# A hybrid decoder step on one core: 24 more weight units of the input projection taken in high and low halves, the low half made by an accumulating DMA

## The chip, the core and the metric

The kernel runs on one core of one Trainium2 chip. Its time is the device time of one execution in microseconds (us); smaller is better. A result is the median of several executions.

## What is computed

Two layers of a decoder trunk, for 256 prompt positions and 8 sample positions together (264 columns). The part that the change touches is the input projection of each layer, `proj = xn @ w_in`, and beside it the state-space scan and the search for the cut of the top 256 keys:

```
xn = rmsnorm(x, norm_mix)
proj = xn @ w_in                     # 2048 -> 8448 padded columns
u, q, k, v, qi, ki, wi, gl = jnp.split(proj, ...)
y_att = attend(q, k, v, qi, ki, wi, pos)          # top-256 keys by indexer score
y_ssm, h_re, h_im = s5_scan(u, h0_re, h0_im, a_re, a_im, log_dt, b_re, b_im, c_re, c_im, d)
gates = jax.nn.sigmoid(gl).reshape(nb, s, N_BRANCH, D_MODEL)
x = x + (gates[:, :, 0] * (y_ssm' @ w_branch[0]) + gates[:, :, 1] * (y_att @ w_branch[1])) @ w_out
x = x + (jax.nn.silu(gate) * up) @ w_ffn_down     # gate, up = split(rmsnorm(x) @ w_ffn_up)
```

All inputs and outputs are fp32.

## The kernel before

**Units.** The weights are streamed from DRAM in units of 128 x 1024 fp32 (512 KB): eight 128 x 128 blocks, eight matmuls' worth, against 264 columns. Units 0 to 131 are `w_in` (two units to a block of 128 output columns, so block f is units 2f and 2f+1), 132 to 203 the GLU, branch and output weights. SyncE loads unit u into slot u % 6 of `ring` once unit u-6 is done (`units` reaches u-5); `u_in[u % 6]` tells that it has landed.

**Two ways to multiply.** A plain unit is one fp32 matmul for each block (L608; the trace has two records for each). A split unit (those in `SPLIT`: 8 to 55, fourteen from 92 to 105, all from 132) is three fp32r matmuls for each block (L604, L605, L606): high weights by high activations, high by low, low by high. ScalarE copies the raw unit to fp32r, which makes the high part (`highs_to`, L1021), and VectorE subtracts it from the raw unit, which makes the low part (`lows_to`, L1311). `w_low` lies at the same addresses as `ring`: the low part is written over the raw one. Units 56 to 91 are plain, since VectorE has other work there.

**The stretch around units 56 to 87.** TensorE takes one unit and then one small matmul (L757), the count of the bisection for the top-256 cut: it waits for `count_ready`, which VectorE gives (L1467), and releases `total_ready`, for which VectorE waits (L1484). VectorE works through the scan of the first half of the states (`scan(0, bisect)`, tensor_tensor instructions L1541, L1549, L1550, L1551, later L1584, L1592, L1593) and puts one step of the bisection between two steps of the scan. Loop n of the count follows unit 56+n. ScalarE only evacuates a block's PSUM bank when its two units are done (L1031, from block 34 on L1045 as a tanh); there are four banks. GpSimd issues nothing from the last fetch of indexer keys (eight, behind units of the first part) until the gathers of keys after the scan of the second half (L1867).

Of the kernel before, what the change touches and what calls it, by code (L numbers as in the profile page):

```python
# [10 lines left out]
ALU = mybir.AluOpType  # L11
# [3 lines left out]
P = 128  # L15
# [98 lines left out]
def build(nc, d, o):  # L114
    with ExitStack() as ctx:
# [214 lines left out]
        def unit_w(u):  # L330

            if u in LATE:
                raw, low = (a[:, u % 6, :].rearrange("p (c n) -> p c n", c=2) for a in (ring, wlow))
                return raw, late_high[LATE[u]], low
            at = HIGH_AT[u % 4]
            return ring[:, u % 6, :], (wih if u < G_GLU else wmh)[:, at:at + KT8], wlow[:, u % 6, :]

        def weight(a, u, k):
            return a[:, k // 4, k % 4 * P:k % 4 * P + P] if u in LATE else a[:, k * P:(k + 1) * P]

        def high_free(u):

            if u in LATE:
                return max((n + 1 for n in LATE if n < u and LATE[n] == LATE[u]), default=0)
# [22 lines left out]
        kg_in = [ctx.enter_context(nc.semaphore(f"kg_in{i}")) for i in range(NS)]  # L367
        vg_in = [ctx.enter_context(nc.semaphore(f"vg_in{i}")) for i in range(NS)]
        cleared = []

        def sem(name):
# [39 lines left out]
        count_ready, total_ready = sem("count_ready"), sem("total_ready")  # L411
        ties_counted, ties_placed, picked, picks_placed = sem("ties_counted"), sem("ties_placed"), sem("picked"), sem("picks_placed")
        per_seq_ready, spread_ready, spread_used, gix_ready = (
            sem("per_seq_ready"), sem("spread_ready"), sem("spread_used"), sem("gather_rows_ready"))
        q_spread, v_out = sem("q_spread"), sem("v_out")
# [84 lines left out]
        for layer in range(DEPTH):  # L500
            with nc.Block() as block:
                def landed(u):
                    return 16 * (G_END // 6 * layer + u // 6 + 1)

                def attend_units(u):
                    return (22 * u + 9) // 18
# [77 lines left out]
                def _(pe):  # L584
                    mm = nc.tensor.matmul

                    def unit_part(u, seq, c, full, high, low, k0, n, opens, closes, made=None):

                        if k0 == 0:
                            if opens:  # L590
                                pe.wait_ge(bank_free[seq % 4], seq // 4 + 1)
                            if u in SPLIT:
                                pe.wait_ge(unit_low, lows_by(u))
                            else:
                                pe.wait_ge(u_in[u % 6], landed(u))
                        out = main[seq % 4][:, 0:T]
                        raw, wh, wl = unit_w(u)
                        for k in range(k0, k0 + n):
                            if made:
                                made(8 * c + k)  # L600
                            kk = 8 * c + k
                            starts, stops = opens and k == 0, closes and k == 7
                            if u in SPLIT:
# [163 lines left out]
                    fill(3)  # L767
                    pe.wait_ge(ties_counted, 1)
                    mm(side[0][:, 1:2], same_seq, n_above, start=True, stop=True)
                    mm(side[0][:, 2:3], before_seq, n_equal, start=True, stop=True).then_inc(ties_placed, 1)  # L770
                    fill(1)
                    pe.wait_ge(picked, 1)
                    mm(side[0][:, 3:4], before_seq, prefix[:, P:NK], start=True, stop=True)
                    mm(side[0][0:NS, 4:5], is_seq, above[:, P:NK], start=True, stop=True).then_inc(picks_placed, 1)
                    fill(1)
                    pe.wait_ge(per_seq_ready, 1)
                    for h in range(2):
# [224 lines left out]
                def _(act):  # L1002
# [6 lines left out]
                    def highs_to(last):  # L1009

                        nonlocal next_high
                        while next_high <= last:
                            u = next_high
                            next_high += 1
                            if u not in SPLIT:
                                continue
                            raw, high, _ = unit_w(u)
# [276 lines left out]
                def _(dve):  # L1294
# [194 lines left out]
                    def pick():  # L1489
# [3 lines left out]
                        st.link(tsc(equal, score, tau, 0.0, ALU.is_equal, ALU.add, accum_out=n_equal))  # L1493
                        dve.sem_inc(ties_counted, 1)
                        st.link(v.tensor_tensor_scan(prefix, ones[:, 0:1].to_broadcast([P, NK]), equal, 0.0, ALU.mult, ALU.add))
                        dve.wait_ge(ties_placed, 1)
# [4 lines left out]
                        v.tensor_tensor_scan(prefix, ones[:, 0:1].to_broadcast([P, NK]), above, 0.0, ALU.mult, ALU.add).then_inc(picked, 1)  # L1501
                        dve.wait_ge(picked, 1)
                        lows_to(92)
                        dve.wait_ge(picks_placed, 1)
                        st.mark(v.tensor_copy(by_rank[:, NK:NK + 1], page_row[:]))
# [6 lines left out]
                        st.link(stt(rank_of, ranks, seg_first, rank_of, ALU.is_ge, ALU.mult))  # L1512
                        dve.sem_inc(per_seq_ready, 1)
                        lows_to(93)
# [315 lines left out]
                def _(pool):  # L1830
# [187 lines left out]
```

## Time and profile before

| | us |
|---|---|
| runs of the kernel before | 3126.95, 3127.31, 3134.06 |
| their median | 3127.31 |
| the profiled execution | 3135.18 |
| its span, first to last instruction | 3133.4 |
| TensorE busy (share of the span) | 3058.2 (98%) |
| VectorE, ScalarE, GpSimd busy | 1949.7, 1193.2, 236.4 |
| units 60 to 83 of layer 0, start of 60 to start of 84 | 88.1 |

The profiled execution is 0.25% above the median, and 1.8 us of it lie around the span. Matmuls are pipelined: their recorded durations overlap, so what a unit takes is read from the starts of two matmuls that stand a unit apart, and not from durations. Busy time of a line says what the engine did there; whether it costs time is told by who waits for whom.

### The profile page before, as it was taken

Reading aid. Unit: us, or ns where it says so; the run is one execution under the profiler, and the core shown is the slowest. Engines: PE = TensorE matmul, PEld = TensorE weight load, DVE = VectorE, ACT = ScalarE, POOL = GpSimd, SP = SyncE. Lnnn points to the kernel's source line nnn. Section 1 sums busy time; section 2 is a strip of 40 time slices with the busy share of each in tenths; the row PEclk is TensorE's granted clock in tenths of the full one; section 3 lists DMA queues with packets and bytes.
Section 4 is the critical chain, followed back from the end, with each engine's and each line's share of the span. In section 5 each row is a group of like instructions: output and inputs, shape, how many; then the busy total and the mean of one; then the engine's idle time right before and its main releaser. Section 6 shows DMA issues by size and latency. Waiting matters only on the chain. (4 is left out here: it accounts for less than half of the span.)

```text
span 3133.4 us, 58534 instructions
## 1 busy us (share of the span) xinstructions
PE 3058.2 (98%) x23384; PEld 2895.2 (92%) x23384; DVE 1949.7 (62%) x3387; ACT 1193.2 (38%) x1689; POOL 236.4 (8%) x219
## 2 busy tenths in 40 slices
PE   8999999999999999999999999999999999999999
PEld 7988777999999999999988887788999999999999
DVE  7558769557655545555575686785676555455553
ACT  4440233434545333334334302334445543333332
POOL 4330000300000000000033200004000000000000
PEclk9999999999999999999999999999999999999999
DMA  7444334655555655556554443347455556555564
GB/s 253 160 147 142 121 110 142 225 172 171 192 179 182 200 169 173 181 181 202 188 191 162 143 142 120 106 147 238 159 179 188 182 180 200 168 174 183 179 207 131
DMA packets 147888, 538.06 MB, mean 172 GB/s; under 512 B 19569, under 2 KB 24817, under 8 KB 147217
## 3 DMA queue, kind: packets, MB, share of 16 engines
q1 hardware_dynamic: 137872, 509.50, 48.9%
q0 software_dynamic: 9216, 25.18, 2.6%
q8 instruction: 111, 1.82, 0.2%
q10 hardware_dynamic: 640, 1.16, 0.1%
q14 instruction: 49, 0.39, 0.0%
HBM read 528.56 MB, written 7.21 MB: 171 GB/s over the span
## 5 line engine op out<-in xcount | busy, mean ns | idle before, releaser
L1750 DVE TENSOR_TENSOR w_ffn_low<-ring_ffn,w_ffn_high 128x1024 fp32r<-128x1024 f32 (+1 forms) x480 | 638.5, 1331 | 464.2 <-ACT w_ffn_high L1256 464.2
L985 PE MATMUL main<-x_ffn_high,w_ffn_high 128*128 128x264 f32 x2816 | 799.3, 284 | 0.0
L986 PE MATMUL main<-x_ffn_low,w_ffn_high 128*128 128x264 f32 x2816 | 797.7, 283 | 0.0
L987 PE MATMUL main<-x_ffn_high,w_ffn_low 128*128 128x264 f32 x2816 | 797.3, 283 | 0.0
L1256 ACT ACTIVATE w_ffn_high<-ring_ffn 128x1024 fp32r<-128x1024 f32 (+1 forms) x480 | 547.9, 1142 | 653.6 <-PE main L987 652.5
L986 PEld LDWEIGHTS main<-x_ffn_low,w_ffn_high 128*128 128x128 f32 x2816 | 530.7, 188 | 0.1
L985 PEld LDWEIGHTS main<-x_ffn_high,w_ffn_high 128*128 128x128 f32 x2816 | 530.3, 188 | 0.1
L987 PEld LDWEIGHTS main<-x_ffn_high,w_ffn_low 128*128 128x128 f32 x2816 | 527.8, 187 | 0.0
L608 PE MATMUL main<-xn,ring 128*128 128x264 f32 x2112 | 484.7, 389 | 0.0
L608 PEld LDWEIGHTS main<-xn,ring 128*128 128x128 f32 x2112 | 394.3, 190 | 65.5 <-issue 0.8
L985 PE MATMUL main<-hidden_high,w_ffn_high 128*128 128x264 f32 x1408 | 400.9, 285 | 0.0
L987 PE MATMUL main<-hidden_high,w_ffn_low 128*128 128x264 f32 x1408 | 399.9, 284 | 0.0
L986 PE MATMUL main<-hidden_low,w_ffn_high 128*128 128x264 f32 x1408 | 398.7, 283 | 0.0
L606 PE MATMUL main<-x_high,w_low 128*128 128x264 f32 x992 | 283.4, 286 | 0.0
L985 PEld LDWEIGHTS main<-hidden_high,w_ffn_high 128*128 128x128 f32 x1408 | 265.1, 188 | 0.0
L987 PEld LDWEIGHTS main<-hidden_high,w_ffn_low 128*128 128x128 f32 x1408 | 265.0, 188 | 0.0
L986 PEld LDWEIGHTS main<-hidden_low,w_ffn_high 128*128 128x128 f32 x1408 | 264.7, 188 | 0.0
L1311 DVE TENSOR_TENSOR w_low<-ring,w_mid_high 128x1024 fp32r<-128x1024 f32 x144 | 175.5, 1225 | 94.3 <-ACT w_mid_high L1021 87.8
L604 PE MATMUL main<-x_high,w_in_high 128*128 128x264 f32 x768 | 226.2, 294 | 4.6 <-DVE w_low L1311 4.3
L605 PE MATMUL main<-x_low,w_in_high 128*128 128x264 f32 x768 | 218.1, 284 | 0.0
L1021 ACT ACTIVATE w_mid_high<-ring 128x1024 fp32r<-128x1024 f32 x144 | 150.6, 1051 | 101.5 <-PE main L606 89.9
L606 PEld LDWEIGHTS main<-x_high,w_low 128*128 128x128 f32 x992 | 188.9, 190 | 0.0
(373 smaller groups left out, 4614.8 us busy)
## 6 DMA issues: line engine op xcount, KB each, us to landing
ring_ffn<-in_w_up SPq DMA_DIRECT2D x352, 512.0 KB, 3.2
ring<-in_w_in SPq DMA_DIRECT2D x264, 512.0 KB
ring_ffn<-in_w_down SPq DMA_DIRECT2D x128, 704.0 KB, 4.1
ring<-in_w_br SPq DMA_DIRECT2D x64, 512.0 KB
ring<-in_w_out SPq DMA_DIRECT2D x64, 512.0 KB
ring<-in_w_glu SPq DMA_DIRECT2D x16, 512.0 KB
out_x<-x SPq DMA_DIRECT2D x8, 528.0 KB, 5.8
x<-in_x SPq DMA_DIRECT2D x4, 528.0 KB, 5.3
```

The costliest lines, as they stand in the source:

```text
L604: mm(out, weight(wh, u, k), high[:, kk, :], start=starts, stop=False)
L605: mm(out, weight(wh, u, k), low[:, kk, :], start=False, stop=False)
L606: m = mm(out, weight(wl, u, k), high[:, kk, :], start=False, stop=stops)
L608: m = mm(out, weight(raw, u, k), full[:, kk, :], start=starts, stop=stops)
L985: mm(out, wfh[:, slot, w], high[:, kk, :], start=kk == 0, stop=False)
L986: mm(out, wfh[:, slot, w], low[:, kk, :], start=False, stop=False)
L987: m = mm(out, wfl[:, slot, w], high[:, kk, :], start=False, stop=kk == chunks * kts - 1)
L1021: af(high, raw, ACT.Copy).then_inc(unit_high, 1)
L1256: af(wfh[:, s, 0:cols], ring_ffn[:, s, 0:cols], ACT.Copy).then_inc(high_ready, 1)
L1311: tt(low, raw, high.bitcast(F32), ALU.subtract).then_inc(unit_low, 1)
L1750: tt(wfl[:, s, 0:cols], ring_ffn[:, s, 0:cols], wfh[:, s, 0:cols].bitcast(F32), ALU.subtract).then_inc(low_ready, 1)
```

## The change

Units 60 to 83 of each layer (`ADDED`) become split units. VectorE has no part in it. ScalarE writes the high part (fp32r copy) into a buffer of its own, and then the negated copy (scale -1) over the raw unit in its slot; that releases `less_high`. GpSimd issues a DMA for each unit which reads the raw unit from DRAM a second time and adds it (`accum_op=ALU.add`) onto the negated highs, so that the slot holds raw minus high, the low part. Its end releases `low_added[u % 2]`, on which TensorE starts the unit. The DMA of unit u waits for the end of that of unit u-2. There are three buffers for highs; unit u from 63 on may be taken by ScalarE when `units` reaches u-2, which is when unit u-3 is done. In `evac_gates` ScalarE now makes the highs of up to unit 2f+4 before it evacuates block f. The other lines of the diff put several semaphores into one (`pick_step`, `placed`), with the same order of waits.

```diff
+ADDED = range(60, 84)
...
+            if u in ADDED and u % 3 == 2:
+                raw, low = (a[:, u % 6, :].rearrange("p (c n) -> p c n", c=2) for a in (ring, wlow))
+                return raw, late_high[0], low
+            at = HIGH_AT[2 + u % 3 if u in ADDED else u % 4]
...
         def high_free(u):
 
+            if u in ADDED:
+                return u - 2 if u >= ADDED[3] else 56
...
+                def added_by(u):
+                    return 16 * (len(ADDED) // 2 * layer + (u - ADDED[0]) // 2 + 1)
...
+                            if u in ADDED:
+                                pe.wait_ge(low_added[u % 2], added_by(u))
+                            elif u in SPLIT:
...
-                            if u in SPLIT:
+                            if u in SPLIT or u in ADDED:
                                 mm(out, weight(wh, u, k), high[:, kk, :], start=starts, stop=False)
...
-                            af(high, raw, ACT.Copy).then_inc(unit_high, 1)
+                            if u in ADDED:
+                                af(high, raw, ACT.Copy)
+                                af(low, raw, ACT.Copy, scale=-1.0).then_inc(less_high, 1)
+                            else:
+                                af(high, raw, ACT.Copy).then_inc(unit_high, 1)
...
                     def evac_gates(first, count):
                         for f in range(first, first + count):
+                            highs_to(min(2 * f + 4, ADDED[-1]))
                             act.wait_ge(units, 2 * f + 2)
...
+                    for u in ADDED:
+                        n = u - ADDED[0]
+                        pool.wait_ge(less_high, n + 1)
+                        if n >= 2:
+                            pool.wait_ge(low_added[u % 2], added_by(u - 2))
+                        g.dma_start(unit_w(u)[2], d["w_in"][layer, u] if u % 3 < 2 else d["w_in"][layer, u].rearrange("p (c n) -> p c n", c=2),
+                                    accum_op=ALU.add).then_inc(low_added[u % 2], 16)
                     pool.wait_ge(gix_ready, 1)
```

ScalarE's instructions in layer 0, from the last split unit before the stretch into the evacuations of blocks 28 and on. Before:

```order
L1021 ACTIVATE w_in_high<-ring 128x1024 [waits units_done,unit_weights_in1,pi_done]
L1115 ACTIVATE arena<-side 128x264 [waits bu_ready] x20
L1031 ACTIVATE proj<-main 128x264 [waits units_done]
L1115 ACTIVATE arena<-side 128x264 [waits bu_ready] x12
L1031 ACTIVATE proj<-main 128x264 [waits units_done] x7
```

And in the changed kernel (its line 1049 is L1031 of before; `main` is the PSUM bank of a block):

```order
L1134 ACTIVATE arena<-side 128x264 [waits bu_ready] x12
L1049 ACTIVATE proj<-main 128x264 [waits units_done]
L1036 ACTIVATE w_in_high<-ring 128x1024 [waits units_done,unit_weights_in0]
L1037 ACTIVATE w_low<-ring 128x1024
L1049 ACTIVATE proj<-main 128x264 [waits units_done]
L1036 ACTIVATE w_in_high<-ring 128x1024 [waits units_done,unit_weights_in1]
L1037 ACTIVATE w_low<-ring 128x1024
L1036 ACTIVATE w_in_high_b<-ring 128x2x512 [waits units_done,unit_weights_in2]
L1037 ACTIVATE w_low<-ring 128x1024
L1049 ACTIVATE proj<-main 128x264 [waits units_done]
```

Between two evacuations there now stand two pairs of copies, one pair for each unit. On GpSimd, behind the last fetches of keys, before:

```order
L1858 AFFINE_SELECT arena<-arena 128x128 [waits pi_acc]
L1839 DMA arena<-in_kidx,arena 128x128 [waits units_done] x8
L1867 DMA bbt<-in_ck,gix 128x512 [waits y_ready,units_done,pa_out_copied,gather_rows_ready]
L1867 DMA bbt<-in_ck,gix 128x512
L1867 DMA bbt<-in_ck,gix 128x512 [waits units_done]
```

And in the changed kernel, where 24 DMAs stand there, of which the first five are shown:

```order
L1877 AFFINE_SELECT arena<-arena 128x128 [waits pi_acc]
L1858 DMA arena<-in_kidx,arena 128x128 [waits units_done] x8
L1887 DMA w_low<-in_w_in 128x1024 [waits less_high] x2
L1887 DMA w_low<-in_w_in 128x1024 [waits low_added0,less_high]
L1887 DMA w_low<-in_w_in 128x1024 [waits low_added1,less_high]
L1887 DMA w_low<-in_w_in 128x1024 [waits low_added0,less_high]
```

The gathers of keys come behind all 24 on this queue.

## Rows read from the trace of the kernel before

**Rows 1.** The page: busy time by engine (us, share of the span, instructions).

```profile
PE 3058.2 (98%) x23384; PEld 2895.2 (92%) x23384; DVE 1949.7 (62%) x3387; ACT 1193.2 (38%) x1689; POOL 236.4 (8%) x219
```

**Rows 2.** Timeline of TensorE, units 56, 57, 60 and 84: start, us, instruction.

```profile
223.91 3.72 PE L608 MATMUL main<-xn,ring 128*128 128x264 f32 x16
227.28 0.36 PE L757 MATMUL side<-n_over_r,same_seq_r 128*128 128x2 f32 x1
...
230.95 0.36 PE L757 MATMUL side<-n_over_r,same_seq_r 128*128 128x2 f32 x1
231.17 3.81 PE L608 MATMUL main<-xn,ring 128*128 128x264 f32 x16
...
238.51 3.81 PE L608 MATMUL main<-xn,ring 128*128 128x264 f32 x16
...
326.63 3.81 PE L608 MATMUL main<-xn,ring 128*128 128x264 f32 x16
```

**Rows 3.** Timeline of TensorE: first matmuls of two split units that follow each other.

```profile
48.02 0.28 PE L604 MATMUL main<-x_high,w_in_high 128*128 128x264 f32 x1
...
50.94 0.28 PE L604 MATMUL main<-x_high,w_in_high 128*128 128x264 f32 x1
```

**Rows 4.** Who waited for whom, 227.3 to 341.1 us: total us, times, longest.

```profile
ACT arena L1045 <- PE main L608: 61.1, 9, 7.0
ACT proj L1031 <- PE main L608: 41.6, 6, 7.0
DVE cut L1484 <- PE side L757: 9.5, 15, 1.7
```

**Rows 5.** Timeline of VectorE: steps of the bisection in the early and the late scan.

```profile
231.75 0.22 DVE L1484 TENSOR_SCALAR cut<-side,cut 128x1 uint32<-128x1 f32 x1
...
235.32 0.22 DVE L1484 TENSOR_SCALAR cut<-side,cut 128x1 uint32<-128x1 f32 x1
...
304.81 0.22 DVE L1484 TENSOR_SCALAR cut<-side,cut 128x1 uint32<-128x1 f32 x1 [0.53 <-PE side L757]
...
308.48 0.22 DVE L1484 TENSOR_SCALAR cut<-side,cut 128x1 uint32<-128x1 f32 x1 [0.53 <-PE side L757]
```

**Rows 6.** Timeline of ScalarE: an evacuation at 231.34, two copies to fp32r.

```profile
231.34 0.39 ACT L1031 ACTIVATE proj<-main 128x264 f32<-128x264 f32 x1 [6.84 <-PE main L608]
...
350.81 1.06 ACT L1021 ACTIVATE w_in_high_b<-ring 128x1024 fp32r<-128x1024 f32 x1 [1.69 <-DVE hs L1595]
351.77 1.04 ACT L1021 ACTIVATE w_in_high_v<-ring 128x1024 fp32r<-128x1024 f32 x1
```

**Rows 7.** Unit 132's last matmul, and the gather that waits for it.

```profile
565.58 0.28 PE L606 MATMUL main<-y_high,w_low 128*128 128x264 f32 x1
...
566.14 1.41 POOL L1867 DMA_INDIRECT arena<-in_cv,gix  x1 [7.83 <-PE main L606]
```

**Rows 8.** GpSimd's gathers (256 KB each), and SyncE's 512 KB loads: issue to landing.

```profile
L1867 POOL DMA_INDIRECT arena<-in_cv,gix x32: 943/964/1730, 566.1 to 2192.9; - x32
...
DMA to landing us min/median/max: 3.9/4.7/5.8
...
ring_ffn<-in_w_up SPq DMA_DIRECT2D x352, 512.0 KB, 3.2
```

**Rows 9.** Windows: us, busy by engine, granted clock, DMA share, GB/s.

```profile
6.00:10.00 4.00, 0.00 (x0) 0.00 (x0) 3.78 (x7) 3.60 (x5) 3.22 (x5) 1.00 1.04 415
242.00:286.00 44.00, 44.00 (x206) 37.76 (x205) 40.74 (x110) 3.63 (x7) 0.00 (x0) 1.00 0.44 144
```

**Rows 10.** Timelines: a key fetch of GpSimd, and VectorE beside it.

```profile
155.62 1.94 POOL L1839 DMA_INDIRECT arena<-in_kidx,arena  x1 [0.98 <-PE side L712]
...
155.51 1.22 DVE L1311 TENSOR_TENSOR w_low<-ring,w_in_high 128x1024 fp32r<-128x1024 f32 x1
```

**Rows 11.** Windows with gaps on TensorE, columns as in rows 9.

```profile
364.00:368.00 4.00, 2.31 (x9) 1.00 (x7) 3.31 (x11) 1.34 (x2) 0.00 (x0) 1.00 0.40 131
368.00:372.00 4.00, 2.89 (x13) 2.92 (x14) 2.44 (x5) 0.00 (x0) 0.00 (x0) 0.64 0.00 0
420.00:424.00 4.00, 3.41 (x34) 2.60 (x27) 1.23 (x1) 2.86 (x8) 0.00 (x0) 1.00 0.40 131
476.00:480.00 4.00, 2.55 (x16) 1.97 (x15) 3.86 (x10) 1.45 (x5) 0.00 (x0) 1.00 0.37 124
```

More of the change, by code:

```diff
@@ L334, in unit_w @@
                 return raw, late_high[LATE[u]], low
-            at = HIGH_AT[u % 4]
+            if u in ADDED and u % 3 == 2:
+                raw, low = (a[:, u % 6, :].rearrange("p (c n) -> p c n", c=2) for a in (ring, wlow))
+                return raw, late_high[0], low
+            at = HIGH_AT[2 + u % 3 if u in ADDED else u % 4]
             return ring[:, u % 6, :], (wih if u < G_GLU else wmh)[:, at:at + KT8], wlow[:, u % 6, :]
         def weight(a, u, k):
-            return a[:, k // 4, k % 4 * P:k % 4 * P + P] if u in LATE else a[:, k * P:(k + 1) * P]
+            halved = u in LATE or u in ADDED and u % 3 == 2
+            return a[:, k // 4, k % 4 * P:k % 4 * P + P] if halved else a[:, k * P:(k + 1) * P]
         def high_free(u):
+            if u in ADDED:
+                return u - 2 if u >= ADDED[3] else 56
             if u in LATE:
-                return max((n + 1 for n in LATE if n < u and LATE[n] == LATE[u]), default=0)
+                return max((n + 1 for n in LATE if n < u and LATE[n] == LATE[u]), default=ADDED[-1] + 1)
             if u < 12:
@@ L368, in build @@
         vg_in = [ctx.enter_context(nc.semaphore(f"vg_in{i}")) for i in range(NS)]
+        low_added = [ctx.enter_context(nc.semaphore(f"low_added{i}")) for i in range(2)]
         cleared = []
@@ L411, in build @@
         count_ready, total_ready = sem("count_ready"), sem("total_ready")
-        ties_counted, ties_placed, picked, picks_placed = sem("ties_counted"), sem("ties_placed"), sem("picked"), sem("picks_placed")
-        per_seq_ready, spread_ready, spread_used, gix_ready = (
-            sem("per_seq_ready"), sem("spread_ready"), sem("spread_used"), sem("gather_rows_ready"))
+        pick_step, placed = sem("pick_step"), sem("picks_placed")
+        less_high = sem("less_high")
+        spread_ready, spread_used, gix_ready = (
+            sem("spread_ready"), sem("spread_used"), sem("gather_rows_ready"))
         q_spread, v_out = sem("q_spread"), sem("v_out")
@@ L767, in _ @@
                     fill(3)
-                    pe.wait_ge(ties_counted, 1)
+                    pe.wait_ge(pick_step, 1)
                     mm(side[0][:, 1:2], same_seq, n_above, start=True, stop=True)
-                    mm(side[0][:, 2:3], before_seq, n_equal, start=True, stop=True).then_inc(ties_placed, 1)
+                    mm(side[0][:, 2:3], before_seq, n_equal, start=True, stop=True).then_inc(placed, 1)
                     fill(1)
-                    pe.wait_ge(picked, 1)
+                    pe.wait_ge(pick_step, 2)
                     mm(side[0][:, 3:4], before_seq, prefix[:, P:NK], start=True, stop=True)
-                    mm(side[0][0:NS, 4:5], is_seq, above[:, P:NK], start=True, stop=True).then_inc(picks_placed, 1)
+                    mm(side[0][0:NS, 4:5], is_seq, above[:, P:NK], start=True, stop=True).then_inc(placed, 1)
                     fill(1)
-                    pe.wait_ge(per_seq_ready, 1)
+                    pe.wait_ge(pick_step, 3)
                     for h in range(2):
@@ L1014, in highs_to @@
                             next_high += 1
-                            if u not in SPLIT:
+                            if u not in SPLIT and u not in ADDED:
                                 continue
-                            raw, high, _ = unit_w(u)
+                            raw, high, low = unit_w(u)
                             act.wait_ge(u_in[u % 6], landed(u))
@@ L1500, in pick @@
                         st.link(tt(above, above, equal, ALU.add))
-                        v.tensor_tensor_scan(prefix, ones[:, 0:1].to_broadcast([P, NK]), above, 0.0, ALU.mult, ALU.add).then_inc(picked, 1)
-                        dve.wait_ge(picked, 1)
+                        v.tensor_tensor_scan(prefix, ones[:, 0:1].to_broadcast([P, NK]), above, 0.0, ALU.mult, ALU.add).then_inc(pick_step, 1)
+                        dve.wait_ge(pick_step, 2)
                         lows_to(92)
-                        dve.wait_ge(picks_placed, 1)
+                        dve.wait_ge(placed, 2)
                         st.mark(v.tensor_copy(by_rank[:, NK:NK + 1], page_row[:]))
@@ L1512, in pick @@
                         st.link(stt(rank_of, ranks, seg_first, rank_of, ALU.is_ge, ALU.mult))
[L1513 removed]
+                        dve.sem_inc(pick_step, 1)
                         lows_to(93)
```

5 lines of the change are left out of this document (2 added, 3 removed).

## The prediction, made before the changed kernel ran

> **What bounds the kernel now.** I read the page's busy times first. TensorE is busy for 98% of the span [rows 1], so the first question for any stretch is what TensorE does there. The timeline of TensorE gives the stretch that the change touches: unit 60 of layer 0 starts at 238.51 and unit 84 at 326.63, 88.1 us for 24 units, 3.67 us a unit [rows 2]. Of a unit's 3.67 us, 0.22 belong to the count matmul that follows it (230.95 to 231.17), which leaves 3.45 for the fp32 matmuls. The list of waits for this stretch has no TensorE row: TensorE waits for nothing there. ScalarE waits for 103 us of it, and VectorE waits for the count, 9.5 us in 15 waits [rows 4]. So the matmuls themselves are the bound, with VectorE close behind. How close is seen in its timeline: early in the scan one step of scan and bisection takes 3.57 us with no wait in it (231.75 to 235.32), and late in the scan 3.67 with a wait of 0.53 in it, thus 3.14 alone [rows 5].
>
> **What is removed.** A split unit takes 2.92 us on TensorE (48.02 to 50.94) [rows 3]. With the count that is 3.14 in place of 3.67, 0.53 less. For 24 units in each of two layers the matmuls give back 48 x 0.53 = 25.4 us. That is the most that the change could bring, and it doesn't reach it, since VectorE's count then comes last. Units 60 to 70 run beside the early steps of 3.57 us and units 71 to 83 beside steps that are no longer than about 3.14, but for two of 3.3 to 3.4 at the change from one kind to the other (estimate, by the widths of the operands). TensorE can't pass the count that VectorE has not given. So the stretch takes at least 11 x 3.57 + 13 x 3.14 + 0.4 = 80.5 us: 7.6 less than now in a layer, 15.2 in both. This is the best case, with low parts that are always ready.
>
> **What is added, and when the low part is ready.** From unit 63 on, ScalarE may write the highs of unit u only when unit u-3 is done. From there a chain runs to the start of unit u, and I call its length L. It has these links.
>
> - End of unit u-3 to ScalarE's start: 0.2. The evacuation at 231.34 starts 0.17 behind the next unit's start at 231.17 [rows 2, 6].
> - Two copies of 128 x 1024, one behind the other: 2.0. The two that stand together in the trace start 0.96 apart, and the second takes 1.04 [rows 6]. I take the copy with scale -1 to cost what the other does.
> - ScalarE to GpSimd: 0.3. GpSimd starts a gather 0.28 behind the end of the matmul that releases it (565.86 to 566.14) [rows 7].
> - The DMA, from the start of GpSimd's issue until it has landed: D, below.
> - Landing to TensorE's first matmul: 0.1 (estimate; no row has it alone).
>
> So L = 2.6 + D. TensorE meanwhile has only units u-2 and u-1 to do. A chain of three units closes on itself: the end of unit u-3, then L, then unit u itself, 2.92. Three units therefore take at least C = L + 2.92 = D + 5.5 us. Units 60, 61 and 62 are made ready early, since their highs wait only for unit 55; they take 3.57 each by VectorE's pace, so unit 62 ends 3.57 + 3.57 + 2.92 = 10.1 behind the start of unit 60. Unit 83 is seven turns of the chain behind unit 62, and one count follows. The stretch then takes 10.1 + 7C + 0.2 us, or the 80.5 above if that is more. It equals the 88.1 of now at C = 11.1, that is D = 5.6 us. Everything hangs on D.
>
> **The price of D.** The trace has no accumulating DMA, and none of GpSimd's that isn't a gather. The nearest rows are the gathers: 256 KB each, issued by GpSimd, 3.9 us from issue to landing at least, 4.7 in the median, 5.8 at most [rows 8]. SyncE's plain load of 512 KB lands 3.2 us after its issue [rows 8], so the path by GpSimd is the slower one to start. A saturated DMA system moved 415 GB/s [rows 9]. The new DMA has twice a gather's bytes, and it can't add without reading the old value: it reads 512 KB from DRAM and 512 KB from the slot and writes 512 KB. Low end: the reads cost as one pass and it lands like the fastest gather, 3.9 + 256 KB / 415 = 4.5 us. High end: both reads and the write one after the other on the same engines, from the slowest gather: 5.8 + 1280 KB / 415 = 9.0; and if GpSimd is held up at each issue by another us, 10. That it can be held up is seen where a fetch of keys took 1.94 us in place of 0.95, while VectorE ran an instruction of 1.22 with two operands from SBUF [rows 10]; the scan consists of such instructions, though shorter ones (0.4 to 0.7 us). I take the middle way that the operation itself suggests, two reads, the write beside them: 4.7 + 768 KB / 415 = 6.6 us. The value is nearest to the median gather row.
>
> It fits what the DMA engines can do. Now they are 44% busy at 144 GB/s [rows 9]. One load of 512 KB for a unit is 1.26 us of a saturated system, and the accumulate with two passes 2.5, together 3.8 us for a unit. The chain gives 4.0 (below), so the DMA engines are then nearly full, which speaks for a D above the low end, and not for one below.
>
> The Trainium skill, Collectives: The Full Stack, section "The bandwidth ceiling: the fold count and why AG ≠ RS ≠ AR", says that an add in the DMA engines halves the rate because it needs two source reads, and not because of the adding. By that rule D is the value with two reads, which I took from the operation; no row here shows it.
>
> **The sum.** L = 9.2, C = 12.1: 10.1 + 84.7 + 0.2 = 95.0 us for the stretch in place of 88.1, 6.9 more in a layer and 13.8 in both. TensorE then stands idle for some 1.4 us once in three units, besides the short waits for VectorE's count. Such gaps don't touch the clock: windows with 0.6 to 1.5 us of idle time in 4 have a granted clock of 1.00 (2.4 GHz); it was 0.64 in a window that followed one with 1.7 us idle, and was itself idle for 1.1 [rows 11]. What follows the stretch moves as a whole: VectorE's scan is tied to TensorE through the count and shifts with it, and the key gathers, which now stand behind the 24 DMAs on GpSimd's queue, are wanted only some 200 us later. ScalarE has the time for 48 more copies (4.4 us of 8 for two units) and the evacuations are covered by four banks. Merged semaphores cost nothing; their waits stay in the same order. Against the profiled execution's 3135.2 the sum gives 3149; it is 0.25% above the median of the runs, and by the median, 3127.3 + 13.8, I predict 3141 us.
>
> **Rivals.**
>
> 1. *The low parts are early enough, VectorE's count becomes the bound, and the kernel is faster.* This needs D under 5.6 us. For it speaks that the fastest gather would give 4.5 and that a plain read path alone, 4.7 + 0.6 = 5.3, would do; against it, that a DMA with an add moves three times 512 KB while the ring loads run beside it. At D = 5.3: C = 10.8, the stretch is 85.9, 2.2 less, and the kernel 4 us faster, 3123. At D = 4.5 the stretch is at the floor of 80.5, and the kernel at 3112. The Trainium skill, DMA: Bandwidth & Descriptors, section "Anatomy of one DMA — SWDGE (gpsimd) path", gives such a DMA 2.0 us and its bytes at 436 GB/s. By that rule even 1 MB would land in 4.4 us and the floor would be reached. The gathers of 256 KB disagree with it here, with 4.7 us in the median where the rule has 2.6 [rows 8]. The chance is 0.28, two thirds of it for a gain of over 9.4 us.
>
> 2. *The accumulating DMA is much slower than its bytes.* Each descriptor's add, the conversion to fp32r or GpSimd's writing of the descriptors holds it up. At D = 9: C = 14.5, stretch 111.8, +23.7 a layer, 3175. At D = 10: +30.7 a layer, 3189. Idle gaps would then be 3 to 5 us in three units, and the clock may fall as it did at 368 us [rows 11], which would add more. For it speaks the stretched issue of 1.94 us [rows 10]; against it, that the scan's instructions are half as long or shorter. Chance 0.26.
>
> 3. *VectorE is held up by GpSimd's issues.* If each issue of 0.95 us blocked the scan, its step would be 4.5 us and the stretch 24 x 4.5 = 108, +20 a layer, 3167. Against it: VectorE's 1.22 us instruction beside the issue at 155.62 kept its length [rows 10]. It lies within the range of rival 2, chance 0.03. That the change doesn't do what it says (the 24 units stay plain) is out: the order of instructions shows them split.
>
> **The numbers.** A measurement of this kernel can tell some 0.3%, 9.4 us, from no change. The forecast (two passes, D from 5.6 to 8, 0 to +33 us) has 0.43: 0.14 of it lies within 9.4 us of now and 0.29 above. Rival 1 gives 0.18 to faster and 0.10 to same. Rivals 2 and 3 give 0.29 to slower. Together faster 0.18, same 0.24, slower 0.58. The range reaches from the floor, 3112, to D = 10, 3189; beyond it, a D over 10 and a fallen clock, is left out.
>
> **What would show it.** The time from the start of unit 60 to that of unit 84 should be some 95 us in place of 88.1; three units some 12.1 us. TensorE's waits should name the DMA onto the low parts, in about seven long gaps a layer, of 1 to 2 us each. The issue-to-landing time of the new DMAs should be 6 to 7 us and the DMA share in the stretch 0.9 or more. A stretch of 80 to 86 us, with waits on VectorE's count alone, would prove rival 1. A landing time of 9 us or more is rival 2. Scan steps over 3.7 us with no wait in them are rival 3. A split unit of more than 2.92 us, by a lower clock, would make the sum wrong in another place.

## The result: 49 us slower, and the profile after

The changed kernel takes 3176.32 us (median of 4 runs, 3170.79 to 3179.07) beside 3127.13 for the kernel before (4 runs): 49 us more by the two medians. The ratio worked out for the two kernels is 1.0146, 95% interval 1.0134 to 1.0158, or some 46 us more. The prediction had 3141, 14 us more. The direction was right and the size three and a half times too small. The profiled execution of the changed kernel took 3170.79, its span 3169.0.

The page's busy times, and its chain of work that ended last, answer to [rows 1]:

```profile
PE 3050.6 (96%) x23768; PEld 2908.6 (92%) x23768; DVE 1947.8 (61%) x3387; ACT 1285.9 (41%) x1785; POOL 269.8 (9%) x267
...
PE main L999 8%; PE main L1000 8%; PE main L1001 8%; PE main L622 4%; PE main L618 4%; PE main L619 3%; PE main L620 3%; DMA w_low<-in_w_in 2%; DVE tmp L1560 1%; DVE w_low L1330 1%; ACT w_mid_high L1039 0%; DVE arena L1568 0%; PE side L745 0%; PE side L758 0%; PE side L726 0%
```

TensorE is 7.6 us less busy, although the split units should have taken 25 us from it, and it is busy for 96% of the span where it was for 98%. A new link stands in the chain: the DMA onto `w_low`. The same pages have the packets, MB and share of the 16 DMA engines of GpSimd's queue, before and after:

```profile
q0 software_dynamic: 9216, 25.18, 2.6%
...
q0 software_dynamic: 16128, 50.35, 6.9%
```

That is 81.5 us of work for all 16 engines before (2.6% of 3133.4) and 218.7 now (6.9% of 3169.0): 2.9 us for each of the 48 new DMAs.

Now the stretch. Unit 60 of layer 0 starts at 238.46 and unit 84 at 348.27: 109.8 us, where it was 88.1 [rows 2] and 95.0 was predicted. In layer 1 it is 109.9. The two stretches together are 43.5 us longer, which is nearly the whole. Windows of the changed kernel (us, busy by engine, granted clock, DMA share, GB/s), the whole stretch and then one gap, the unit behind it and the next:

```profile
238.46:348.27 109.81, 85.42 (x603) 84.74 (x601) 75.42 (x214) 46.97 (x55) 18.12 (x21) 0.88 0.91 225
...
262.42:266.04 3.62, 0.01 (x1) 0.04 (x1) 3.45 (x10) 2.28 (x3) 0.18 (x1) 1.00 1.04 261
266.04:270.60 4.56, 4.56 (x26) 4.56 (x26) 1.05 (x3) 0.00 (x0) 0.86 (x1) 0.63 1.04 252
270.60:273.62 3.02, 3.02 (x28) 3.02 (x27) 2.63 (x7) 2.01 (x2) 0.49 (x1) 1.00 0.88 239
```

The DMA share was 0.44 [rows 9] and is 0.91. The granted clock was 1.00 throughout; now it is 0.63 in the unit behind the gap, and 1.00 again in the next. The timeline of TensorE shows the same turn: units 64 and 65 (256.18, 259.20), the count, then unit 66 behind its gap, and unit 67:

```profile
256.18 0.37 PE L618 MATMUL main<-x_high,w_in_high 128*128 128x264 f32 x1
...
259.20 0.37 PE L618 MATMUL main<-x_high,w_in_high_b 128*128 128x264 f32 x1
...
262.20 0.17 PE L771 MATMUL side<-n_over_r,same_seq_r 128*128 128x2 f32 x1
266.04 0.52 PE L618 MATMUL main<-x_high,w_in_high 128*128 128x264 f32 x1 [3.67 <-DMA w_low<-in_w_in]
...
270.60 0.37 PE L618 MATMUL main<-x_high,w_in_high 128*128 128x264 f32 x1
```

Unit 64 takes 3.02 us with its count, unit 66 takes 4.56. The chain of the prediction can be read link by link, from ScalarE's and GpSimd's timelines:

```profile
256.41 1.06 ACT L1036 ACTIVATE w_in_high<-ring 128x1024 fp32r<-128x1024 f32 x1 [6.41 <-PE main L620]
257.37 1.04 ACT L1037 ACTIVATE w_low<-ring 128x1024 fp32r<-128x1024 f32 x1
...
258.71 0.86 POOL L1887 DMA_DIRECT2D w_low<-in_w_in  x1 [5.76 <-ACT w_low L1037]
```

Unit 63 ends at some 256.2, the copies start at 256.41, GpSimd issues at 258.71, and TensorE starts unit 66 at 266.04, 7.3 us after the issue. The line of the 48 new DMAs, and the waits from 220 to 400 us (answering to [rows 4]):

```profile
L1887 POOL DMA_DIRECT2D w_low<-in_w_in x48: 842/862/1007, 226.6 to 1914.9; - x48
...
DMA to landing us min/median/max: 5.2/6.9/8.8
```

```profile
DVE cut L1503 <- PE side L771: 33.3, 13, 6.3
...
PE main L618 <- DMA w_low<-in_w_in: 24.3, 8, 3.7
```

TensorE waits for the new DMA 24.3 us in layer 0, in eight gaps with 3.7 at most. In layer 1 there are seven, of 3.1 to 4.3 us. VectorE waited 9.5 us for TensorE's count and now waits 33.3. Its own steps are as long as before: 3.56 us from one to the next (answering to [rows 5]), though an issue of GpSimd's stands at 273.13 in the middle of it:

```profile
270.88 0.22 DVE L1503 TENSOR_SCALAR cut<-side,cut 128x1 uint32<-128x1 f32 x1 [3.76 <-PE side L771]
...
274.44 0.22 DVE L1503 TENSOR_SCALAR cut<-side,cut 128x1 uint32<-128x1 f32 x1
```

### The profile page after: what moved, and what is told of

Same layout as the page of the kernel before. It is cut to its first block and busy times, and to the rows that moved or that the text cites. A ratio compares the mean times of both kernels' runs of the same rounds, so it can differ in the third digit from the quotient of the medians.

```text
span 3169.0 us, 59542 instructions
## 1 busy us (share of the span) xinstructions
PE 3050.6 (96%) x23768; PEld 2908.6 (92%) x23768; DVE 1947.8 (61%) x3387; ACT 1285.9 (41%) x1785; POOL 269.8 (9%) x267
## 3 DMA queue, kind: packets, MB, share of 16 engines
q8 instruction: 114, 1.87, 0.2%
## 5 line engine op out<-in xcount | busy, mean ns | idle before, releaser
L620 PE MATMUL main<-x_high,w_low 128*128 128x264 f32 x1376 | 400.9, 291 | 0.0
L618 PE MATMUL main<-x_high,w_in_high 128*128 128x264 f32 x1024 | 312.8, 305 | 53.5 <-DMA w_low<-in_w_in 48.9
L622 PE MATMUL main<-xn,ring 128*128 128x264 f32 x1344 | 308.7, 387 | 0.0
L619 PE MATMUL main<-x_low,w_in_high 128*128 128x264 f32 x1024 | 301.3, 294 | 0.0
L622 PEld LDWEIGHTS main<-xn,ring 128*128 128x128 f32 x1344 | 252.1, 190 | 42.0 <-issue 0.8
L620 PEld LDWEIGHTS main<-x_high,w_low 128*128 128x128 f32 x1376 | 269.9, 196 | 0.0
L618 PEld LDWEIGHTS main<-x_high,w_in_high 128*128 128x128 f32 x1024 | 203.5, 199 | 69.0 <-issue 32.0
```

## The experiments

Three explanations were to be told apart: the time that one accumulating DMA takes on its path (latency), the work that all of them put on the DMA engines beside the ring loads (capacity), and the clock behind the gaps. For each kernel the table gives the time, the ratio to the kernel before on the same chip, the change against it (3131.18, median of 16 runs, for the first four, 3131.68, 21 runs, for the others; for the change itself also 3131, since its own four runs of before, 3127, are few: with them it is +49), and two views: the length of the stretch in both layers, less the 176.2 us of before, and the issue-to-landing time of the new DMAs, median. The last column is worked out from the pages, as above: the work of GpSimd's queue (its share times the span), less the 81.5 us of before, divided by the number of the new DMAs; it is good to 0.1 us.

| kernel | time, us | ratio (95%) | change | stretches | landing | DMA work of one |
|---|---|---|---|---|---|---|
| the change | 3176.32 | 1.0146 (1.0134 to 1.0158) | +45 | +43.5 | 6.9 | 2.9 |
| no accumulate | 3112.62 | 0.9944 (0.9928 to 0.9961) | -18.6 | -19.9 | | |
| plain copy | 3141.43 | 1.0035 (1.0020 to 1.0050) | +10.3 | +14.8 | 4.1 | 1.7 |
| no ring loads | 3140.56 | 1.0027 (1.0014 to 1.0040) | +9.4 | +13.3 | 5.5 | 3.1 |
| gaps filled | 3165.48 | 1.0115 (1.0098 to 1.0132) | +34.3 | +37.7 | 7.3 | 3.0 |
| three in flight | 3175.25 | 1.0139 (1.0123 to 1.0155) | +43.6 | +44.1 | 7.5 | 2.9 |
| two of three units | 3127.65 | 0.9993 (0.9984 to 1.0002) | -4.0 | -1.1 | 8.0 | 2.8 |
| one of two units | 3119.80 | 0.9965 (0.9951 to 0.9978) | -11.9 | -12.0 | 7.2 | 2.8 |
| no ring loads, gaps filled | 3134.53 | 1.0013 (1.0004 to 1.0023) | +2.9 | +5.6 | 5.5 | 3.0 |

The two columns of changes agree within 5 us, so the time is lost and won in the stretches. The first is of medians over several executions and the second of one execution; those of the kernel before alone go from 3124 to 3136 us (21 runs), those of the plain copy from 3128 to 3150 (10 runs).

### No accumulate

```diff
                            if u in ADDED:
-                                pe.wait_ge(low_added[u % 2], added_by(u))
+                                pe.wait_ge(less_high, u - ADDED[0] + 1)
...
-                    for u in ADDED:
-                        n = u - ADDED[0]
-                        pool.wait_ge(less_high, n + 1)
-                        if n >= 2:
-                            pool.wait_ge(low_added[u % 2], added_by(u - 2))
-                        g.dma_start(unit_w(u)[2], d["w_in"][layer, u] if u % 3 < 2 else d["w_in"][layer, u].rearrange("p (c n) -> p c n", c=2),
-                                    accum_op=ALU.add).then_inc(low_added[u % 2], 16)
```

> The 24 accumulating DMAs of each layer are left out: the low parts stay negated highs (the product of these units is not the reference's), and TensorE starts an added unit when ScalarE's two copies are done. Theory A (the changed kernel loses by the chain highs, DMA, unit, which closes every three units, and by the clock that falls in the gap at its end): without the DMA the chain is 2.6 + 2.9 = 5.5 us for three units, no gap, granted clock 1.00; the stretch from the start of unit 60 to that of unit 84 takes 80 to 81 us (VectorE's count is the bound), against 88.1 before and 109.8 in the changed kernel, and the kernel some 15 us under the kernel before, about 3112. Rival B (the split units themselves, ScalarE's 48 extra copies or VectorE's slowed scan cost the time): the stretch stays above 88 and the kernel is slower than before.

The 24 DMAs of a layer are left out, and the low part is minus the high part. The stretch in layer 0:

```profile
237.56:315.71 78.15, 75.54 (x603) 73.22 (x601) 74.77 (x214) 47.03 (x55) 0.00 (x0) 1.00 0.49 162
```

78.2 us, 2.3 less than the floor of 80.5: the first four units went at 3.03, and only then came VectorE's 3.57, which it kept until unit 72. So the removed matmul time, the copies of ScalarE and the merged semaphores were priced rightly, the whole loss lies in the DMA, and the DMA has a price of 64 us (3176.3 less 3112.6).

### Plain copy in place of the add

```diff
                         g.dma_start(unit_w(u)[2], d["w_in"][layer, u] if u % 3 < 2 else d["w_in"][layer, u].rearrange("p (c n) -> p c n", c=2),
-                                    accum_op=ALU.add).then_inc(low_added[u % 2], 16)
+                                    ).then_inc(low_added[u % 2], 16)
```

> The same 48 DMAs from GpSimd, but without the add: they write the raw weights over the negated highs (the low part is the raw weight, so the product of these units is not the reference's). The slot is then not read by the DMA. Theory A with two reads as the cause of the long DMA: issue to landing falls from 6.9 us in the median to about 5.3, on the chain from 7.3 to 5.5; the chain is 11 us for three units, the gap and with it the low clock are all but gone, the stretch 85 to 88 us, the kernel 3115 to 3127. Rival C (what is slow is the path by GpSimd, or the conversion to fp32r, not the add): landing stays at 6.9, the stretch near 110 and the kernel near 3176.

The DMA overwrites the slot with the raw weights. GpSimd's issue now takes 0.53 us in place of 0.86, and the landing 4.1 in the median:

```profile
237.68:336.19 98.51, 81.13 (x602) 80.52 (x601) 75.45 (x214) 47.00 (x55) 11.09 (x21) 0.91 0.74 246
```

```profile
DMA to landing us min/median/max: 3.5/4.1/8.0
```

The add alone thus costs 35 us (3176.3 less 3141.4). GpSimd's queue has 5.2% of the engines' time here:

```profile
q0 software_dynamic: 16128, 50.35, 5.2%
```

One such DMA puts 1.7 us of work on the DMA engines, the one with the add 2.9 us, 1.7 times as much, for the same bytes read from DRAM. But even the plain copy leaves the kernel 10 us slower than before. In layer 0 its gaps were long and short in turn: unit 63 waited 4.03, unit 69 waited 3.87, and unit 66 between them 0.67. The DMA of unit 63 was issued at 243.24 and had landed at 250.89, 7.7 us later, beside ring loads with a DMA share of 1.03 (246 to 250 us); that of unit 66, issued at 258.00, took 4.2. Why the long ones stand where they do stays open; in layer 1 they stand at other units, and the stretch took 92.5 us there.

### No ring loads beside it

```diff
-                        sp.dma_start(ring[:, u % 6, :], d[src][layer, n]).then_inc(u_in[u % 6], 16)
+                        cols = 16 if u in ADDED and u >= 63 else KT8
+                        sp.dma_start(ring[:, u % 6, 0:cols], d[src][layer, n][:, 0:cols]).then_inc(u_in[u % 6], 16)
...
+                                if u >= 63:
+                                    raw = xn[:].rearrange("p k t -> p (k t)")[:, 0:KT8]
...
```

> SyncE's 512 KB loads of units 63 to 83 are cut to 8 KB each, and ScalarE makes its copies from other data of the same size (the product of these units is not the reference's); the accumulating DMAs are as in the changed kernel. The accumulates then have the DMA engines to themselves. Theory D (the engines are saturated by ring loads and accumulates together, share 1.03 in the gaps, and that sets the landing time of 7.3 on the chain): landing falls to about 5.5, the gap to under 1 us with a full clock, the stretch to 85 to 90, the kernel to 3115 to 3130. Rival (the accumulate is slow by itself): landing stays near 7, the stretch near 105 to 110, the kernel near 3170.

The units 63 to 83 are computed from other numbers, with 8 KB loaded for each.

```profile
237.38:332.35 94.97, 79.02 (x602) 78.05 (x601) 75.61 (x215) 46.98 (x55) 18.16 (x21) 0.95 0.83 152
```

```profile
DMA to landing us min/median/max: 5.3/5.5/9.0
```

Minimum and median are now nearly one: 5.5 us is what this DMA takes with no ring load beside it, though up to two of its kind are under way at a time. The median of 6.9 in the changed kernel holds 1.4 us of contention with the ring loads, and without that contention, and with the shorter gaps that this leaves, the kernel is 36 us faster. The gap ahead of unit 81 is the longest of layer 0, 4.09 us: the full loads of units 84 and on begin when unit 78 is done. A D of 5.5 us is just under the prediction's break-even of 5.6, yet the kernel lost 9 us, which leads to the clock: a gap of 2.54 us ahead of unit 66 was followed by a unit of 4.56. Its own price on the DMA engines did not fall: 3.1 us of work for each.

### The gaps filled with matmuls

```diff
                             if u in ADDED:
+                                if u >= 63 and u % 3 == 0:
+                                    for _ in range(28):
+                                        mm(side[1][:, 0:T], xh[:, 0, 0:P], xh[:, 0, :], start=True, stop=True)
                                 pe.wait_ge(low_added[u % 2], added_by(u))
```

> TensorE does 28 more fp32r matmuls of 264 columns (3.4 us) into a PSUM bank that nobody reads, ahead of its wait for the low part of units 63, 66, ... 81, where it is idle in the changed kernel. Nothing else changes, and the output is the same. Theory A (the gap of 3.7 us lowers the granted clock to 0.5 for 3.6 us, and the unit behind it takes 4.5 us in place of 2.9, which is part of the chain): clock 1.00 in the stretch, units of 2.9 us, the chain 14.1 down to 12.6, the stretch 109.8 down to about 99, the kernel some 21 us faster than the changed one, about 3155. Rival D (the chain's length is the DMA engines' work for three units, three loads and three accumulates, so a faster unit only waits longer): clock 1.00, but the stretch and the kernel's time as in the changed kernel, 3176.

```profile
238.05:345.04 106.99, 99.31 (x799) 98.37 (x797) 75.58 (x214) 47.12 (x55) 18.16 (x21) 0.98 0.96 232
```

```profile
DMA to landing us min/median/max: 5.3/7.3/10.4
```

The clock came back, from 0.88 to 0.98, and with it split units at full speed behind the places of the gaps. Seven units a layer at 1.5 us would be 21 us. The kernel won 11, and the stretches 6. Two things stood against the rest. One is the edit itself: the 28 matmuls take 3.4 us each time, also where the low part is there sooner. For unit 72 the DMA was issued at 284.48 and landed 5.4 us later, at 289.9, and TensorE was still at the dummies:

```profile
289.82 2.68 PE L607 MATMUL side<-x_high 128*128 128x264 f32 x21
292.34 0.29 PE L621 MATMUL main<-x_high,w_in_high 128*128 128x264 f32 x1
```

Units 66, 72, 75 and 78 of layer 0 began 1.9, 2.5, 2.9 and 4.9 us after their low part had landed (1.2 of the last are unit 77's own matmuls). The other is the DMA engines, which are still fuller (0.91 to 0.96): the landing goes from 6.9 to 7.3 in the median and from 8.8 to 10.4 at most. By the profile's share they have 0.91 x 109.8 = 100 us of work in the stretch of the changed kernel and 0.96 x 107.0 = 103 here, and the share is 1.04 where they are saturated. So a stretch under 96 us was probably not to be had with this change, however early the DMAs were issued (an estimate from these shares). The stretch before took 88.

### Three DMAs in flight

```diff
-        low_added = [ctx.enter_context(nc.semaphore(f"low_added{i}")) for i in range(2)]
+        low_added = [ctx.enter_context(nc.semaphore(f"low_added{i}")) for i in range(3)]
...
-                        if n >= 2:
-                            pool.wait_ge(low_added[u % 2], added_by(u - 2))
+                        if n >= 3:
+                            pool.wait_ge(low_added[u % 3], added_by(u - 3))
...
```

> Edit: three semaphores in place of two for the accumulating DMAs, so that the DMA of unit u waits for that of unit u-3 and not u-2; the rest is the changed kernel's. Theory A (the chain runs from the end of unit u-3 by the copies and the DMA's own landing, and the wait of GpSimd for the DMA before is not on it, since the three units of a bunch are wanted one after the other): nothing moves, ratio within 0.2% of the changed kernel's 1.015, some 3176 us, a stretch of 109 to 110 us. Rival (GpSimd's wait for the DMA of unit u-2 delays the issue of the one that TensorE waits for, or three transfers at once share the DMA engines to the same end but let the first start earlier): the gaps ahead of units 63, 66 and so on shrink by 1 us or more each, and the kernel is 14 us or more faster, 3162. The third way: three transfers beside each other slow the one that is wanted first; then it is slower, by up to 1 us a gap, 3190.

The third DMA of a bunch is issued earlier (that of unit 65 at 249.82 in place of 252.08), and no longer waits for a landing:

```profile
249.82 0.86 POOL L1887 DMA_DIRECT2D w_low<-in_w_in  x1 [2.63 <-ACT w_low L1037]
```

The time did not move (3175 beside 3176), and the landing went to 7.5 us. GpSimd's wait for the DMA before, 61 us in the changed kernel, cost nothing. That fits DMA engines that are the limit by the bytes that they carry and not by their issue.

### Fewer units

```diff
-ADDED = range(60, 84)
+ADDED = [u for u in range(60, 84) if u % 3 != 2]
```

```diff
-ADDED = range(60, 84)
+ADDED = [*range(60, 84, 2)]
```

Where the code counted by u, u % 2 or u % 3, both count by a unit's place in this list.

> Edit: only the units of 60 to 83 with u % 3 != 2 (16 of the 24) are split by copies and accumulating DMA, the others stay plain as before. Theory A (the DMA engines' work, one accumulate of some 2.6 us and one load of 1.3 us for a unit, and the chain over three buffers are both too long for units of 2.9 us, and the clock falls in the gaps): for three units the DMA engines now have 2 x 2.6 + 3 x 1.3 = 9.1 us of work in about 10.2, and the chain of 2.6 + 7.3 us has 3.5 units of TensorE's work (11.8 us) beside it. So no gaps, full clock, and TensorE or VectorE's count is the bound: some 11 x 3.6 + 13 x 3.32 = 82.8 us for the stretch in place of 88.1, thus 3117 us, with 3112 to 3122 as bounds, faster than both kernels. Theory D (an accumulating DMA among the ring loads costs TensorE a gap whenever it is waited for): two thirds of the loss stays, some +33 us, 3160.

> Edit: only the even units of 60 to 83 (12 of the 24) are split by copies and accumulating DMA, the odd ones stay plain. Theory A: DMA engines with 2.6 + 2 x 1.3 = 5.2 us of work in 6.8, chain with six units' time: no gap, full clock; the stretch is 12 x 3.14 + 12 x 3.67 = 81.7 us by TensorE, a little more where VectorE's early steps of 3.57 bind, some 83.5; 4.6 us less than before in a layer, 3118 us, 3115 to 3123. If e6 is free of gaps, e7 is slower than it by up to 2 us; if e6 still has some, e7 is the faster. Theory D: half of the loss stays, +25 us, 3152.

Two of three, then one of two, layer 0:

```profile
237.41:323.71 86.30, 78.88 (x538) 74.00 (x537) 75.99 (x215) 33.29 (x41) 12.06 (x14) 1.00 0.92 238
```

```profile
238.46:321.37 82.91, 80.80 (x506) 74.16 (x505) 75.88 (x214) 25.74 (x33) 8.63 (x10) 1.00 0.84 221
```

With two of three the expectation of 3117 was missed by 11 us. I had worked out 9.1 us of DMA work for three units in 10.2 and called that free of gaps. With 1.6 us for a load (0.44 of 88.1 us for 24 of them, before) and 2.8 for an accumulate it is 10.4, which leaves nothing; the share was 0.92, the landing 8.0 us, longer than in the change itself, and TensorE had gaps of 0.5 to 1.8 us. The clock stayed at 1.00, and the kernel is equal to the one before. At nine tenths of the DMA engines the landing time isn't that of the DMA alone any more.

With one of two the kernel is the fastest here of those that leave nothing out: 11.9 us faster than before, 0.9965 (0.9951 to 0.9978), expected 3118 and measured 3119.8. The one larger gap of layer 0 (1.38 us, unit 66) has another cause, seen in ScalarE's timeline:

```profile
250.20 1.06 ACT L1037 ACTIVATE w_in_high<-ring 128x1024 fp32r<-128x1024 f32 x1 [4.48 <-DMA ring<-in_w_in]
```

The raw unit itself came late. Its slot was free when unit 60 ended, at 241.5, and the load, which takes 3.2 us elsewhere [rows 8], was there only at 250.2. So contention works in both directions: the accumulates also delay the ring loads, and with a ring of six slots the chain then is load, copies and DMA together.

### No ring loads and the gaps filled

```diff
+                        cols = 16 if u in ADDED and u >= 63 else KT8
...
+                                if u >= 63 and u % 3 == 0:
+                                    for _ in range(16):
+                                        mm(side[1][:, 0:T], xh[:, 0, 0:P], xh[:, 0, :], start=True, stop=True)
...
```

> Edit: the changed kernel with the ring loads of units 63 to 83 cut to 8 KB each, ScalarE taking its input from the activations (so these units multiply other numbers), and with 16 further matmuls on TensorE ahead of the wait of units 63, 66, 69 and so on, whose result nobody reads. It joins the two edits that were made apart before: without ring loads 3141 us, with the gaps filled 3165, the changed kernel 3176. Theory A (DMA engines shared and the clock after gaps are two causes, and all of the loss): landing 5.3 to 5.5 us, units of 2.92 us, three units 2.6 + 5.4 + 2.92 = 10.9 to 11.3 us, a stretch of 87 to 89 us, 3127 us, within 5 of the kernel before. Rival (something else slows the chain): it stays at some 3135 to 3141.

Both edits together, with 16 dummy matmuls in place of 28 (units 63 to 83 are computed from other numbers, as above).

```profile
238.55:330.74 92.19, 88.20 (x715) 86.88 (x713) 75.81 (x214) 47.07 (x55) 18.16 (x21) 1.00 0.85 157
```

```profile
DMA to landing us min/median/max: 5.2/5.5/7.8
```

The first five turns of layer 0 (three units each, counted from the end of unit 62) took 11.2, 11.2, 11.8, 11.2 and 11.4 us. The prediction's formula, D + 5.5, gives 11.0 for the measured 5.5. The last two, 12.7 and 13.6, again run beside the full loads from unit 84 on; they make up most of what the stretch has over the expected 87 to 89. The kernel is 2.9 us over the one before, where the change is 45 over it. So slow landing beside ring loads and the clock behind the gaps, both on the chain of three buffers, account for 42 of the 45 us.

## Why the prediction was right or wrong

**What bounds the kernel, what is removed, and the floor** held. Without the DMA the stretch is 78.2 us where 80.5 was the floor; TensorE's split unit takes 3.02 us with its count where 3.14 was taken; ScalarE's two copies, its start and GpSimd's start took 2.5 us together where I had 2.5.

**The chain was the right mechanism.** The gaps come once in three units (13.8 to 14.4 us apart in layer 0, but for one that is split between units 78 and 79), they name the DMA onto the low parts, and the formula C = D + 5.5 gives nearly what is measured where the clock stays up and the DMA engines have room (11.2 to 11.8 us against 11.0, in the last experiment). Its terms were mis-sized. Unit 62 ended 9.2 us behind the start of unit 60 (predicted 10.1). The seven turns up to the end of unit 83 then took 100.4 us, 14.3 each (predicted 84.7, 12.1 each): 15.7 less 0.9 is the 14.8 us by which the stretch exceeds 95.0.

**The step that failed was "such gaps don't touch the clock".** It failed in its input first. I put TensorE's idle time at 1.4 us a turn, which is 12.1 less three units at VectorE's pace of 3.57. But a chained turn has no such pace: during the gap VectorE works off its steps, and the units then run at 3.03. The idle time of a predicted turn was 12.1 - 9.1 = 3.0 us in one piece. [rows 11] were windows with 0.6 to 1.5 us of idle time and did not answer for that; the row that did was there, 1.7 us of idle time in one window and 0.64 in the next, and I gave it to rival 2. In the changed kernel 13 of the 15 gaps were 3.0 to 4.3 us and the unit behind them took 4.3 to 4.6 us in place of 3.03, and 5.5 at unit 75 of both layers. That is some 1.6 of the 2.2 us a turn (estimate: the 11.4 us that the units of layer 0 took over full speed, in seven turns). The last sign in the prediction, a split unit of more than 2.92 us by a lower clock, is the one that appeared.

**D was 7.0 on the chain where I had 6.6** (the mean of the 15 DMAs that TensorE waited for, 6.9 in layer 0 and 7.1 in layer 1; 5.6 to 7.9), 0.3 to 0.5 of the 2.2 us. The 7.3 of unit 66 holds the 0.1 from landing to first matmul, and one of the longer landings. Without ring loads D is 5.5, below my middle value and just under break-even; so the price of the add was right in kind (the DMA work is 1.7 times that of a plain copy), and its surroundings were not priced. The Trainium skill, Collectives: The Full Stack, section "The bandwidth ceiling: the fold count and why AG ≠ RS ≠ AR", says that an add halves the rate by its two source reads; this case's 2.9 beside 1.7 us comes near to that, though not to the full factor of two, and no run here separates the reads from the adding. The rule of the Trainium skill, DMA: Bandwidth & Descriptors, section "Anatomy of one DMA — SWDGE (gpsimd) path" (2.0 us and the bytes at 436 GB/s), gives 3.2 us for the plain copy of 512 KB, and here that took 3.5 at least and 4.1 in the median.

**The DMA engines' budget was worked out from the wrong row.** I took 1.26 us for a load (512 KB at 415 GB/s) and 3.8 for load and accumulate together, and read "nearly full" out of it as a mere support for D. The share of the same window said more: 0.44 of 88.1 us for 24 loads is 1.6 us each. With the 2.9 measured for the accumulate it is 4.5 for a unit, or 4.3 at a share of 1.04, more than the 3.67 that a unit took before; even with my own 2.5 for two passes it is 4.1, or 3.9. By that estimate the change could not win, whatever D was by itself, and rival 1, at 0.28, had a row against it that I had not priced. A load's price is less certain than the sum: the saturated window of [rows 9] gives 1.3 (512 KB at 415 GB/s, share 1.04), by which the unit still comes to 4.0 with the measured 2.9.

**The rivals.** Rival 1 (D under 5.6) fell with the ring loads beside it. Rival 2 had the right time, 3175, for D = 9, but by luck and not by its reason: D was 7.0, and no issue was held up; 0.86 us in the median of the 48 and 1.01 at most, beside VectorE's scan. Its sentence on the fallen clock is what happened, at a smaller D. Rival 3 is out: VectorE's steps kept their 3.57 us.

**What stays open.** How much of the loss is capacity and how much latency can't be split cleanly, since each edit moves the other: filling the gaps raised the landing time, and the dummies held some units up themselves. A kernel with more than three buffers of highs was not tried, for want of room; by the estimate of capacity above it could have reached 96 us a stretch, still slower than before. Five of the kernels (plain copy, no ring loads, gaps filled, two of three, both edits together) lie 3 to 5 us under what their stretches say, against a spread of 9 to 22 us over the executions of each; the cause stays open, with one execution of each profiled.

## What to carry to other kernels

Before work is handed to a DMA, add up the busy share of the DMA engines for the stretch: share times length divided by transfers gives the price of one (1.6 us for a 512 KB load here), and an accumulating one cost 1.8 times that here. Where loads and accumulates together brought the share to 0.84 and more, the landing times of both grew, and a chain over few buffers grows with them. The share alone doesn't tell it: at 0.83 and 0.85 without the loads the landing stayed at 5.5 us. An offload that loses in full may win in part: half of the units gave 12 us where all of them cost 45 to 49. And if a chain makes TensorE idle, price the idle time in one piece, a turn less the matmuls alone, and the slower unit behind it too.

## What the runs showed of the hardware that was not expected

- An accumulating DMA of 512 KB from DRAM onto SBUF, issued by GpSimd, lands 5.5 us after its issue (median) with no loads beside it, 6.9 beside loads of 512 KB for each unit; a plain one beside the same loads 4.1. Its issue takes 0.86 us in place of 0.53.
- It occupies the DMA engines for 2.9 us, a plain one for 1.7. The page counts its bytes once (GpSimd's queue moved 25.2 MB more, 48 x 512 KB).
- Beside VectorE's scan these issues stayed at 0.86 us, though the indirect fetch in [rows 10] had been stretched to 1.94.
- After every gap of 2.16 us and more in these stretches the granted clock was 0.50 (1.2 GHz) in the unit behind it, a step of 0.22 us between two matmuls. In most it came back to 1.00 (2.4 GHz), a step of 0.12, before the unit's end; at unit 75 of the changed kernel, in both layers, it was 0.50 to the end. After gaps up to 1.7 us, in the stretches of all kernels here, the next unit ran at full speed, 2.9 us from its first matmul to its last. Between them it differed: 1.79 (two of three units), 1.81 (the change), 1.87 and 2.04 (no ring loads) were followed by a unit at full speed, but 1.77 by one of 4.0, 1.89 by one of 4.3 and 1.91 by one of 4.4 (all no ring loads). The window in the middle of unit 66 of the changed kernel:

```profile
267.00:269.00 2.00, 2.00 (x11) 2.00 (x11) 0.12 (x1) 0.00 (x0) 0.29 (x1) 0.50 1.05 285
```
